# Routing of the first token tile between the pieces of the out projection, with the top-4 choice by match-replace

## The reference

```
h = RMSNorm(x);  p = h @ W_in                 # conv branch and gated linear attention
x = x + concat(y_conv, y_gla) @ W_out         # the out projection
h = RMSNorm(x)
logits = h @ W_router + b_router              # 32 experts
top_v, top_i = top_k(logits, 4);  gates = softmax(top_v)
for each expert e: out_e = ((up + 1) * glu) @ W_down[e] + b_down[e],
    with gate, up from h @ W_gate_up[e] + b_gate_up[e], clamped at 7
x = x + sum over the 4 chosen of gate * out_e
out = RMSNorm(x, norm_final_g)
```

## Time and profile before

| | us |
|---|---|
| median of 3 runs | 1087.28 (1085.97 to 1087.99) |
| the profiled execution's own time | 1087.49 |
| its span, first to last instruction | 1085.6 |
| TensorE busy | 1017.5 (94% of the span) |
| VectorE busy | 239.7 |
| ScalarE busy | 144.0 |
| DMA, share of 16 engines (large queue) | 92.4% |
| mean granted TensorE clock | 0.991 of 2.4 GHz |

### The profile page before, as it was taken

One profiled execution on the slowest core, in us unless ns is written; L12 is line 12 of the kernel. 1 busy time (PEld: TensorE's weight loads), 2 busy tenths in 40 slices (PEclk: granted clock), 3 DMA queues, 4 the chain that ended last, 5 costly groups with the idle time before them and its releaser, 6 DMA issues.

```text
span 1085.6 us, 10840 instructions
## 1 busy us (share of the span) xinstructions
PE 1017.5 (94%) x4646; PEld 397.1 (37%) x4646; DVE 239.7 (22%) x614; ACT 144.0 (13%) x282; POOL 9.9 (1%) x26
## 2 busy tenths in 40 slices
PE   6999979999999999999999989999999999999995
PEld 5588543333333333333333323333333323333331
DVE  1253122222222222222222212211211212112213
ACT  2211021111111111111111111111111111111112
POOL 2000000000000000000000000000000000000000
PEclk9999989999999999999999999999999999999998
DMA  9724687999999999999999999999999999999993
GB/s 372 291 101 155 267 337 279 427 427 427 428 426 427 426 427 428 426 425 425 429 427 426 427 428 427 426 427 426 427 427 426 427 427 427 428 426 426 427 427 148
DMA packets 30512, 423.54 MB, mean 390 GB/s; under 512 B 3696, under 2 KB 3968, under 8 KB 4864
## 3 DMA queue, kind: packets, MB, share of 16 engines
q1 hardware_dynamic: 29520, 422.06, 92.4%
q10 hardware_dynamic: 944, 0.77, 0.2%
HBM read 421.77 MB, written 1.05 MB: 389 GB/s over the span
## 4 chain that ended last, share of the span: by engine, by line
PE 60%; DMA 37%; DVE 2%; issue 1%; ACT 1%; another core or an unknown queue 0%; PEldq 0%; SPq 0%; DVEq 0%; ACTq 0%
DMA ring<-in_w_down 32%; PE bank L1089 22%; PE bank L1102 15%; PE bank L901 7%; DMA ring<-in_w_gate_up 5%; PE bank L1035 4%; PE bank L1153 3%; PE bank L986 3%; PE bank L1118 2%; PE bank L897 1%; PE bank L1043 1%; PE bank L1126 1%; DMA x_sb<-in_x 0%; PE bank L1005 0%; PE bank L889 0%
## 5 line engine op out<-in xcount | busy, mean ns | idle before, releaser
L1089 PE MATMUL bank<-ring,x_t 128*64 128x512 f32 x2048 | 466.1, 600 | 10.5 <-DMA ring<-in_w_gate_up 9.1
L1102 PE MATMUL bank<-ring,act 128*64 128x512 f32 x1024 | 238.6, 597 | 22.1 <-DMA ring<-in_w_down 21.6
L1089 PEld LDWEIGHTS bank<-ring,x_t 128*64 128x64 f32 x2048 | 136.9, 137 | 290.2 <-issue 255.7
L1102 PEld LDWEIGHTS bank<-ring,act 128*64 128x64 f32 x1024 | 70.9, 136 | 159.2 <-issue 157.8
L799 DVE TENSOR_TENSOR gu_b<-bank,bias_t 128x512 f32<-128x512 f32 x64 | 44.3, 692 | 371.0 <-PE bank L1118 371.0
L901 PE MATMUL bank<-h_t,ring 128*128 128x256 f32 x320 | 71.8, 386 | 1.0 <-ACT h_t L436 1.0
L526 ACT COPY gu_sb<-bank 128x512 f32<-128x512 f32 x64 | 37.5, 586 | 238.8 <-PE bank L1089 238.8
L901 PEld LDWEIGHTS bank<-h_t,ring 128*128 128x128 f32 x320 | 61.8, 194 | 10.4 <-ACT h_t L436 1.4
L1035 PE MATMUL bank<-x_sb,p_row 128*64 128x512 f32 x256 | 61.8, 604 | 2.7 <-DVE p_gate L752 2.7
L1153 PE MATMUL bank<-z,p_t 64*128 64x512 f32 x256 | 63.6, 615 | 0.7 <-ACT z L545 0.7
L760 DVE TENSOR_TENSOR x_t<-bank,cols 128x512 f32<-128x512 f32 x32 | 22.1, 691 | 173.8 <-PE bank L1043 173.8
(11 more groups left out here) (173 smaller groups left out, 323.6 us busy)
## 6 DMA issues: line engine op xcount, KB each, us to landing
ring<-in_w_gate_up SPq DMA_DIRECT2D x128, 2048.0 KB, 43.7
ring<-in_w_down SPq DMA_DIRECT2D x64, 2048.0 KB, 44.2
ring<-in_w_in SPq DMA_DIRECT2D x6, 2048.0 KB, 20.9
ring<-in_w_out SPq DMA_DIRECT2D x2, 2048.0 KB, 11.9
x_sb<-in_x SPq DMA_DIRECT2D x2, 512.0 KB, 4.1
out<-y_out SPq DMA_DIRECT2D x2, 512.0 KB, 2.6
g_bc<-in_norm_final_g SPq DMA_DIRECT2D x1, 512.0 KB, 44.7
bias_t<-in_b_gate_up ACTq DMA_DIRECT2D x1, 256.0 KB, 20.6
```

The costliest lines, as they stand in the source:

```text
L1089: ins = mm(bank[h][a * SLOTS:(a + 1) * SLOTS, :], x_t[:, k, :], w[:, kk, a, :], start=k == 0, stop=k == KT - 1)
L1102: ins = mm(bank[0][a * SLOTS:(a + 1) * SLOTS, :], act[:, k, :], w[:, kk, a, :], start=k == 0, stop=k == KT - 1)
```

## The change

The out projection's last half, out(1,1), becomes two pieces of 256 columns, in banks 2 and 7. The transposes of tile 0 move into the middle of out(1,0), its logits, its choice and its ranks between the pieces, and tile 1 is turned in three steps (four, two and two blocks) as its columns come; VectorE copies the last two, ScalarE the others. The sum of squares of tile 1 is taken in three parts, the first two being added ahead. The gather of item 0 is done tile by tile. `choose(t)` finds the four largest with max8, fills the other four needles with a large number, replaces the first occurrence of each needle in the logits by -3e38 (`match_replace`), and takes what differs. The root needs two VectorE steps and not four, and ScalarE forms the variance itself (scale and bias of Ln). For item 0 the rows are placed before the gates are; the counts of the extra items, their table and the sums move into item 0 behind its first, second and third piece of work, and `place_slots` is split in two functions. Lines taken out, which stand above, are left out at "...".

```diff
-        OUT_BANK = (5, 6, 1, 2)
+        OUT_BANK = (5, 6, 1, 2, 7)
+        TURN_BANK = ((0, 3), (0, 6))
...
+            roots = [0]
+            def rsqrt(t, total, plus):
+                roots[0] += 1
+                c = slice(t, t + 1)
+                act_e.activation(lnv[:, c], total, ACT.Ln, scale=1.0 / D, bias=plus).then_inc(s_lv, 1)
+                act_e.wait_ge(s_lv, roots[0])
+                act_e.activation(root[:, c], lnv[:, c], ACT.Exp, scale=-0.5).then_inc(s_rs, 1)
...
+            def keep_x2(n, t, k0, k1, dst_bank):
+                act_e.wait_ge(s_tr, 4 + n + 1)
+                c0 = k0 % 4 * P
+                act_e.copy(h_t[:, k0:k1, t * P:(t + 1) * P],
+                           dst_bank[:, c0:c0 + (k1 - k0) * P].rearrange("p (a t) -> p a t", t=P)).then_inc(s_trA, 1)
+            def square_part(i, c0, c1, junk):
+                act_e.wait_ge(s_x2, 2 + i + 1)
+                act_e.activation(junk, xs[:, 1, c0:c1], ACT.Square, accum_out=ss3[:, i:i + 1]).then_inc(s_ss, 1)
+            act_e.wait_ge(s_x2, 2)
+            square_sum(0, h_t[:, :, P:T])
+            act_e.wait_ge(s_ss, TT + 1)
+            rsqrt(0, ss[:, 0:1], eps_c[:, 0:1])
+            keep_x2(0, 0, 0, 4, bank[0])
+            keep_x2(1, 0, 4, 8, bank[3])
+            square_part(0, 0, 512, h_t[:, 4:8, P:T])
+            keep_x2(2, 1, 0, 4, bank[0])
+            square_part(1, 512, 768, p_t[:, :])
+            keep_x2(3, 1, 4, 6, bank[6])
+            square_part(2, 768, 1024, p_t[:, :])
+            act_e.wait_ge(s_rest, 1)
+            act_e.wait_ge(s_ss, TT + 4)
+            rsqrt(1, ss3[:, 2:3], rest[:, 0:1])
...
+            made = [0]
+            def rstd_of(t, total, plus):
                 c = slice(t, t + 1)
...
+                dve.tensor_scalar(var[:, c], total, -0.5 / D, plus, ALU.mult, ALU.add).then_inc(s_rstd, 1)
+                dve.wait_ge(s_rs, made[0] // 3 + 1)
+                dve.wait_ge(s_rstd, made[0] + 1)
+                dve.scalar_tensor_tensor(out=tmp2[:, c], in0=root[:, c], scalar=root[:, c], in1=var[:, c],
+                                         op0=ALU.mult, op1=ALU.mult).then_inc(s_rstd, 1)
+                dve.wait_ge(s_rstd, made[0] + 2)
+                dve.scalar_tensor_tensor(out=rstd[:, c], in0=tmp2[:, c], scalar=1.5, in1=root[:, c],
+                                         op0=ALU.add, op1=ALU.mult).then_inc(s_rstd, 1)
+                dve.wait_ge(s_rstd, made[0] + 3)
+                made[0] += 3
...
+            def add_out(n, t, c0, c1, src):
+                dve.wait_ge(s_op, n + 1)
+                dve.tensor_tensor(xs[:, t, c0:c1], xs[:, t, c0:c1], src, ALU.add).then_inc(s_x2, 1)
+            def choose(t):
+                link(dve.scalar_tensor_tensor(out=lg[:, t, :], in0=bank[4][:, t * E:(t + 1) * E], scalar=rstd[:, t:t + 1],
+                                              in1=br_bc[:, :], op0=ALU.mult, op1=ALU.add))
+                link(dve.max(out=lmax[:, t, :], in_=lg[:, t, :]))
+                link(dve.tensor_copy(four[:, t, 0:TOP], lmax[:, t, 0:TOP]))
+                link(dve.match_replace(out=left[:, t, :], in_to_replace=four[:, t, :], in_values=lg[:, t, :], imm_value=-BIG))
+                dve.tensor_tensor(chosen[:, t, :], left[:, t, :], lg[:, t, :], ALU.not_equal).then_inc(s_cho, 1)
+            def rank_and_place(t):
+                dve.wait_ge(s_rk, t + 1)
+                link(dve.scalar_tensor_tensor(out=rank1[:, t, :], in0=bank[5][:, t * E:(t + 1) * E], scalar=1.0,
+                                              in1=chosen[:, t, :], op0=ALU.add, op1=ALU.mult))
+                dve.tensor_scalar(p_row[:, t, :], slot1[:, 0:SLOTS], rank1[:, t, 0:1], rstd[:, t:t + 1],
+                                  ALU.is_equal, ALU.mult).then_inc(s_p0, 1)
+            dve.memset(four[:, :, TOP:8], BIG)
+            add_out(0, 0, 0, 512, bank[OUT_BANK[0]][:, :])
+            add_out(1, 0, 512, 1024, bank[OUT_BANK[1]][:, :])
+            dve.wait_ge(s_ss, TT + 1)
+            rstd_of(0, ss[:, 0:1], -0.5 * EPS)
+            add_out(2, 1, 0, 512, bank[OUT_BANK[2]][:, :])
             dve.wait_ge(s_lg, 1)
...
+            choose(0)
+            add_out(3, 1, 512, 768, bank[OUT_BANK[3]][:, 0:256])
+            dve.wait_ge(s_const, 3)
+            rank_and_place(0)
+            dve.wait_ge(s_ss, TT + 3)
+            link(dve.tensor_tensor(rest[:, 1:2], ss3[:, 0:1], ss3[:, 1:2], ALU.add))
+            link(dve.tensor_scalar(rest[:, 0:1], rest[:, 1:2], 1.0 / D, EPS, ALU.mult, ALU.add))
+            dve.tensor_scalar(rest[:, 1:2], rest[:, 0:1], -0.5, None, ALU.mult).then_inc(s_rest, 1)
+            dve.wait_ge(s_rest, 1)
+            add_out(4, 1, 768, 1024, bank[OUT_BANK[4]][:, 0:256])
+            dve.wait_ge(s_tr, 4 + 5)
+            dve.tensor_copy(h_t[:, 6:8, P:T], bank[6][:, 2 * P:4 * P].rearrange("p (a t) -> p a t", a=2)).then_inc(s_trD, 1)
+            dve.wait_ge(s_ss, TT + 4)
+            rstd_of(1, ss3[:, 2:3], rest[:, 1:2])
+            dve.wait_ge(s_lg, 2)
+            choose(1)
+            rank_and_place(1)
+            link(dve.tensor_tensor(ex[:, :, :], lg[:, :, :], lmax[:, :, 0:1].broadcast_to([P, TT, E]), ALU.subtract))
+            dve.sem_inc(s_lgk, 1)
...
+            keep_turned(0)
+            place_gates(0, slot1[:, :])
             dve.tensor_copy(gates4[:, :, :, :], gates[:, :, :].rearrange("p t (a e) -> p t a e", a=1)
                             .broadcast_to([P, TT, SPLITS, E])).then_inc(s_gtk, 1)
+            dve.wait_ge(s_cnt, 1)
+            link(dve.tensor_copy(cnt[:, :], bank[7][0:E, 256:257]))
+            dve.tensor_scalar(more[:, :], block_c[:, :], cnt[:, 0:1], None, ALU.is_lt).then_inc(s_more, 1)
...
+                ks = list(range(CT, KT)) + list(range(CT))
+                for j in js:
+                    k = ks[j]
                     if t == 0 and n == 0 and k in (0, 2):
                         pe.wait_ge(s_yconv, k // 2 + 1)
...
+                    ins = mm(bank[OUT_BANK[2 * t + n + (c0 > 0)]][:, 0:c1 - c0], y_t[:, k, t * P:(t + 1) * P], w[:, k, c0:c1],
                              start=j == 0, stop=j == KT - 1)
...
...
+            every = range(KT)
+            out_project(0, 0, 0, 512, every, True)
+            out_project(0, 1, 0, 512, every, True)
+            out_project(1, 0, 0, 512, range(0, 4), False)
+            pe.wait_ge(s_trA, 2)
+            transpose_x(0, 0, 4, 1)
+            transpose_x(0, 4, 8, 2)
+            out_project(1, 0, 0, 512, range(4, KT), True)
+            pe.wait_ge(s_wr, 1)
+            pe.wait_ge(s_trA, 4)
+            logits(0, 0, KT)
+            out_project(1, 1, 0, 256, every, True)
+            transpose_x(1, 0, 4, 3)
+            pe.wait_ge(s_cho, 1)
+            pe.wait_ge(s_const, 3)
+            mm(bank[5][:, 0:E], before[:, :], chosen[:, 0, :], start=True, stop=True).then_inc(s_rk, 1)
+            pe.wait_ge(s_trA, 5)
+            logits(1, 0, 4)
+            out_project(1, 1, 256, 512, range(0, 4), False)
+            transpose_x(1, 4, 6, 4)
+            out_project(1, 1, 256, 512, range(4, KT), True)
+            pe.wait_ge(s_trA, 6)
+            logits(1, 4, 6)
+            pe.wait_ge(s_op, 5)
+            pe.sem_inc(s_used, 2)
+            transpose_x(1, 6, 8, 5)
+            pe.wait_ge(s_trD, 3)
+            logits(1, 6, 8)
+            pe.wait_ge(s_p0, 1)
+            mm(bank[5][:, E:2 * E], ones[:, :], chosen[:, 0, :], start=True, stop=False)
+            gather([0])
+            pe.wait_ge(s_cho, 2)
+            mm(bank[5][:, E:2 * E], before[:, :], chosen[:, 1, :], start=False, stop=True).then_inc(s_rk, 1)
+            for t in range(TT):
+                ins = mm(bank[7][0:E, 256:257], chosen[:, t, :], ones[:, 0:1], start=t == 0, stop=t == TT - 1)
+            ins.then_inc(s_cnt, 1)
+            pe.wait_ge(s_p0, 2)
+            gather([1])
...
             turn_gathered(0)
...
+            def count_extras():
+                pe.wait_ge(s_gtk, 2)
+                for t in range(TT):
+                    ins = nc.tensor.transpose(bank[6][:, t * P:(t + 1) * P],
+                                              gates4[:, t, :, :].rearrange("p a e -> p (a e)"), ident[:, :])
+                ins.then_inc(s_gt, 1)
+                pe.wait_ge(s_more, 1)
+                mm(bank[7][0:E, 0:nb], before[0:E, 0:E], more[:, :], start=True, stop=True)
+                mm(bank[7][0:E, nb:2 * nb], ones[0:E, 0:E], more[:, :], start=True, stop=True)
+                mm(bank[7][0:1, 64:64 + nb], ones[0:E, 0:1], more[:, :], start=True, stop=True).then_inc(s_pref, 1)
...
+                pe.wait_ge(s_p, it + 1)
                 for t in range(TT):
                     ins = nc.tensor.transpose(bank[3][:, t * P:(t + 1) * P], p_gate[:, t, :], ident[:, :])
                 ins.then_inc(s_pt, 1)
                 if following == 1:
+                    count_extras()
+                gate_up(1, range(4))
+                if following == 1:
+                    fill_table()
+                gate_up(2, range(0, 2))
```

(51 more changed lines are left out.)

136 lines of the change are left out of this document (30 added, 106 removed).

## The result

The changed kernel takes 1079.95 us in the median of 4 runs (1078.99 to 1081.19), against 1087.23 (1085.97 to 1087.99) beside it: ratio 0.9935, 95% interval 0.9918 to 0.9952, so 5 to 9 us less. The forecast was 1079.9. The profiled execution has a span of 1077.6, 8.0 under the other one; part of these 8.0 comes from the clock at the start, as the experiment with the filler there shows.

A forecast was written before the change was run, and what follows sets the result against it. The prediction took the stream of expert loads at 427 GB/s as the bound, with 12.7 us lost in holes between 145.8 and 190. Stream 6.1 (start's 0.7 included) plus tail 1.3 make 7.4 us: 1079.9, range 1077.8 to 1083.5.

The forecast's parts named there:

- Cost 1: Out projection ends 4.4 us later, at 150.1, since TensorE does logits and transposes ahead of that end.
- Cost 2: Router's choice of the four largest: match-replace taken at 0.2 us, the choice at 1.1, on the path only for tile 1.
- The path behind: From the out projection's end to the first product's end: 15.3 us at the low clock, where it was 23.8.
- Which clock: TensorE's clock on the path behind the out projection: taken as low, first product ending at 165.4, not 162.3.
- Rival A: Clock already low in the out projection's second half, doubling it: gain 2.1, about 1085 us; chance 0.13.
- Gain 1: Kernel start: shorter reciprocal roots let the projections start 0.7 us earlier (0 to 1.2).
- Gain 2: Expert load stream: of 12.7 us lost, 5.6 and 1.0 remain; gain 6.1 us, the start's 0.7 included.
- Gain 3: Kernel tail: the last two roots, bare on the path, get shorter by 1.3 us (1.0 to 1.5).
- C: Out projection ends where it did, loads 8 and 9 go at 145.0: 1074.6 us; chance 0.04.
- D: Slower: the path behind the out projection doesn't get shorter, first product ends at 173.2: 1088.1 us; chance 0.04.
- E: TensorE waits for tile 0's choice inside the out projection, whose end moves 2 more: 1081.9 us; chance 0.06.
- B: Clock stays high throughout and no chunk is late: gain 8.4, 1078.9 us; chance 0.25.

The follow-up runs named there:

- the experiment with the filler there: 18 unread matmuls before the first transposes, added to both kernels: changed kernel 1078.10 us, kernel before 1085.04 us.
- the filler in the router: Changed kernel plus six small unread matmuls in TensorE's gaps behind the out projection: 1080.12 us, ratio 0.9933.
- the early load: Changed kernel, but load 8 waits only for the out projection's third product, load 9 for its end as before: 1080.39 us, ratio 0.9939.

## Why the prediction was right, step by step

- **The stream as the bound.** Right. From 190 us on it is 427 GB/s in every kernel, and the rest follows the releases ahead of it: 12.0 and not 15.5 us to load 11 shorten it by 1.4, load 12 held back by 6.8 lengthens it by 5.1. That the two bounds lie as near each other as the sum put them, 164.1 and 164.7, agrees with load 11 at 163.12 against 162.36, but no experiment here measures the distance alone.
- **Cost 1**, 4.4 us: measured 4.3. From the out projection's start to the issue of loads 8 and 9 it is 33.0 us (114.64 to 147.66), where it was 28.7 (117.06 to 145.77). The one wait for ScalarE's copy is there (0.5), and no wait for tile 0's choice.
- **Cost 2**, match-replace at 0.2: 0.27, in two instructions, a value load of 0.09 and the replacement of 0.18, as the Trainium skill says ("VectorE: DVE Perf Modes", section on two Vector instructions with no wait between them). The choice takes 1.2 us from logits to `chosen`, 1.1 in the sum.
- **The path behind**, 15.3 at the low clock: 15.5 (147.66 to 163.12). Two errors cancel: up to the first product it is 9.1 and not 9.9, since the rank product didn't have to wait for the gather's first half (clock still high there), and the first product takes 6.33 and not 5.35. At the high clock the sum had 12.2; the filler in the router gave 12.0, with ScalarE's table load in front of its copy of x_row as assumed.
- **Which clock.** Low as assumed, from 152 to 162. Rival A's cause didn't come: 1.00 from 141 to 149.55, transposes, small products and waits included. The Trainium skill says that transposes don't count as busy for the clock in the same way ("TensorE: Matmul & The Clock Gate", Part 4). In the router that can't be seen, but the start of this kernel speaks against it: TensorE does nothing there but 16 transposes before the first projections, and in the six early starts the projections find the high clock. In the changed kernel the last transposes have it already, 273 ns for one and not 421 (the rows give count, then shortest, median and longest ns; the third is the kernel before, with the late start):
```profile
L908 PE MATMUL bank<-ident,h_row x16: 273/421/448, 8.8 to 12.0; 128*128 128x128 f32 x16
```
```profile
L936 PE MATMUL bank<-h_t,ring x64: 379/379/454, 13.5 to 27.1; 128*128 128x256 f32 x64
```
```profile
L901 PE MATMUL bank<-h_t,ring x64: 379/379/763, 14.1 to 29.6; 128*128 128x256 f32 x64
```
  So the reason that the prediction gave for rival A out of that page doesn't hold for these transposes.
- **Load 11** 0.6 late: 0.8 (163.12 against 147.66 + 14.7). Load 12 followed at 4.4, taken at 4.6; load 13 at 5.8, taken at 5.7.
- **Gain 1**, start 0.7: 0.54 from the arrival of x on (9.55 to 9.01), 0.94 in the pair with the filler. The term was of the right size. By smaller pieces it was large: the scaled row of tile 0 comes 0.2 earlier and not 0.4, that of tile 1 0.9 and not 1.2. What the sum had only in a bracket ("the first passes are slow in any case") is worth more than the term: 1.8 us, in some executions and not in others.
- **Gain 2**, stream 6.1: 12.7 us lost became 5.5, so 7.2. But both are counted from 145.8, and the 1.8 of the start are in it: 5.4 without them, 0.7 less than forecast.
- **Gain 3**, tail 1.3: from the first add's start (1074.13 and 1067.18 in the chains) to the last scaling's end 8.4 became 7.3, so 1.1. The last scaling stands 0.6 behind the other's end as forecast, which gives 0.7; tile 0 gives 0.4 and not 0.6.
- **The sum**, 7.4: 7.3 in the medians, 6.7 in the spans with the filler, 6.2 in the first pair of profiles without the 1.8 of the start. The mechanism and its terms are right to within a microsecond; that the forecast lies 0.05 us from the median is luck, where each kernel's four runs spread over 2 us.
- **The signs.** Loads 8 and 9 were to go out at 149 to 150 and went at 147.66: the cost was right and the start 1.8 earlier. No wait in the out projection was over 0.53 us, no second hole came, and rivals C, D and E came in none of their signs. B's high clock came in the changed kernel only with the filler in the router, and by the rest it was worth 1.4 where B had 1.0.

**What carried it**, in the rests and from the arrival of x: roots 0.5 at the start and 1.1 in the tail; 4.5 in the router, of which the order of the pieces is worth about 3 (2.5 in the medians, 3.3 in the rest). How the other 1 to 2 us divide between the moved sums, the choice and the earlier rows of item 0 isn't shown.

## What to carry to other kernels

Where weights stream through a ring without a break until the end, an edit ahead of the stream is worth what it takes out of the stream's holes, and nothing else: list each load's release, and sum traffic against the full rate. Where two releases may bind at nearly the same height, single edits can measure as next to nothing; try them in pairs, and compare profiles from a common event on, not by whole spans, so that a start that differs by chance isn't taken for an effect. Ahead of a stretch where TensorE must stand in short waits, a few matmuls that nobody reads can hold its clock. When waits become bare, look at what the matmuls behind them take as well: here that was eight times the waits themselves.

## What the runs showed of the hardware that I had not expected

- The clock's rise at the start differs between executions: of the ten profiles without matmuls ahead of the first transposes, four had the first two projections in 15.9 to 16.1 us and six in 14.05. With matmuls from 2.15 us on it was 14.05 in all three; with six of ten without them, three aren't proof.
- Where the start was early, TensorE had done nothing but 16 float32 transposes when its clock rose: 273 ns for the shortest of them, 421 in the median, and no product of 128 x 256 behind them over 454 ns, where the late start has some of 763.
- In the router of the changed kernel TensorE was busy 7.35 of 9.07 us at 0.50 and stayed there until about 162; with the filler it was busy 11.57 of 12.10 at 1.00. The first product took 3.65 us at the high level and 5.35 to 6.61 in the profiles in which the clock had fallen before it; it has no gap inside, and the clock rose only during it or at its end.
- 18 matmuls at the start and six in the router, all superfluous, shorten the kernel: 4.7 us with the early load, of which the early load alone gives nothing that can be told.
